# A fourth buffer of split weights in a two-layer decoder step, and attention's last copies moved ahead of the first output part

## The reference

```python
q = (xn @ wq).reshape(B, T, MEM_HEADS, MEM_HEAD_DIM)
s = jnp.einsum('bthd,bmhd->bhtm', q, k).astype(jnp.float32) * (MEM_HEAD_DIM ** -0.5)
p = jax.nn.softmax(s, axis=-1)
o = jnp.einsum('bhtm,bmhd->bthd', p, v).reshape(B, T, D_MODEL)
return o @ wo
...
for e in range(N_EXPERTS):
    out = out + combine[:, e:e + 1] * swiglu(xt, wg[e], wu[e], wd[e])
```

## Time and profile before

| | |
|---|---|
| the profiled execution | 1164.83 us, span 1163.0 us |
| three runs | 1159.54, 1162.23, 1162.55 us |
| TensorE (PE) busy | 1088.9 us, 94% |
| loading of stationary operands (PEld) busy | 1022.9 us, 88% |
| VectorE (DVE) busy | 794.7 us, 68% |
| ScalarE (ACT) busy | 646.4 us, 56% |
| read from memory | 265.83 MB, 234 GB/s over the span |
| mean granted clock of TensorE | 0.974 |

### The profile page before, as it was taken

How to read it: one execution, slowest core, us unless ns; L and a number is a source line. 1 busy time by engine, 2 the same in 40 slices (tenths; PEclk the granted TensorE clock), 3 DMA queues, 4 the chain that set the end, 5 groups by cost and what they waited for, 6 DMA issues and landing times.

```text
span 1163.0 us, 19968 instructions
## 1 busy us (share of the span) xinstructions
PE 1088.9 (94%) x7698; PEld 1022.9 (88%) x7698; DVE 794.7 (68%) x1121; ACT 646.4 (56%) x864; POOL 21.5 (2%) x40
## 2 busy tenths in 40 slices
PE   6999999899999998998997979999999999999995
PEld 5998987699999998998974979898989999999994
DVE  5598643566555656688623466887888788888883
ACT  5676543464434445675523336775766676676762
POOL 0001000000000000002100000000000000000000
PEclk8999999899999999999999869999999999999998
DMA  8444579746555554544498435996989698979961
GB/s 332 155 147 148 164 273 327 290 153 202 183 179 182 183 171 136 179 146 140 162 330 304 172 121 207 341 375 225 362 295 367 231 359 295 345 250 347 324 249 39
DMA packets 64276, 273.00 MB, mean 235 GB/s; under 512 B 7328, under 2 KB 7584, under 8 KB 63552
## 3 DMA queue, kind: packets, MB, share of 16 engines
q1 hardware_dynamic: 62352, 264.33, 64.2%
q0 software_dynamic: 1408, 7.12, 1.7%
q10 hardware_dynamic: 432, 0.38, 0.1%
HBM read 265.83 MB, written 5.98 MB: 234 GB/s over the span
## 4 chain that ended last, share of the span: by engine, by line
PE 71%; DVE 15%; ACT 7%; DMA 3%; issue 3%; SPq 0%; DVEq 0%; ACTq 0%
PE bank L598 10%; PE bank L595 10%; PE bank L600 10%; PE bank L599 10%; PE bank L596 10%; PE bank L597 10%; DVE wl L1402 4%; DMA ring<-dense 3%; ACT wh L1023 2%; PE bank L623 2%; DVE rstd L1397 2%; DVE wl L1663 2%; DVE sq L1413 1%; PE bank L754 1%; PE bank L878 1%
## 5 line engine op out<-in xcount | busy, mean ns | idle before, releaser
L1663 DVE TENSOR_TENSOR wl<-ring,wh 128x1408 fp32r<-128x1408 f32 x192 | 310.4, 1624 | 56.5 <-ACT wh L1269 56.3
L1402 DVE TENSOR_TENSOR wl<-ring,wh 128x1024 fp32r<-128x1024 f32 x170 | 207.1, 1224 | 198.4 <-ACT wh L1023 197.6
L1269 ACT ACTIVATE wh<-ring 128x1408 fp32r<-128x1408 f32 x189 | 261.0, 1381 | 82.2 <-PE bank L600 81.9
L595 PE MATMUL bank<-xh,wh 128*128 128x264 f32 x928 | 272.9, 294 | 21.3 <-DVE xl L1418 13.7
L1023 ACT ACTIVATE wh<-ring 128x1024 fp32r<-128x1024 f32 x170 | 178.9, 1056 | 172.1 <-PE bank L597 135.1
L596 PE MATMUL bank<-xl,wh 128*128 128x264 f32 x928 | 268.4, 289 | 0.0
L597 PE MATMUL bank<-xh,wl 128*128 128x264 f32 x928 | 267.6, 288 | 0.0
L599 PE MATMUL bank<-wh,xl 128*128 128x352 f32 (+4 forms) x736 | 243.1, 330 | 0.0
L595 PEld LDWEIGHTS bank<-xh,wh 128*128 128x128 f32 x928 | 179.6, 194 | 29.6 <-issue 25.1
L596 PEld LDWEIGHTS bank<-xl,wh 128*128 128x128 f32 x928 | 180.1, 194 | 0.0
L597 PEld LDWEIGHTS bank<-xh,wl 128*128 128x128 f32 x928 | 179.5, 193 | 0.0
(11 more groups left out here) (219 smaller groups left out, 1355.1 us busy)
## 6 DMA issues: line engine op xcount, KB each, us to landing
ring<-experts SPq DMA_DIRECT2D x192, 704.0 KB, 5.9
ring<-dense SPq DMA_DIRECT2D x234, 512.0 KB, 4.0
o_k<-kv POOLq DMA_DIRECT2D x2, 1024.0 KB, 4.5
o_v<-kv POOLq DMA_DIRECT2D x2, 1024.0 KB, 7.6
x<-xT SPq DMA_DIRECT2D x2, 528.0 KB, 4.9
o_y<-sq SPq DMA_DIRECT2D x4, 264.0 KB, 2.1
gatew<-gate_w POOLq DMA_DIRECT2D x2, 512.0 KB, 8.2
mem<-memT SPq DMA_DIRECT2D x1, 1024.0 KB, 13.3
```

The costliest lines, as they stand in the source:

```text
L595: mm(out, s_hi, m_hi, start=start, stop=False)
L1269: A(wh[:, jj % NBUF, :], eraw(jj % ESLOTS), ACT.Copy).then_inc(ehi_ready, 1)
L1402: V.tensor_tensor(wl[:, k % NBUF, 0:UNIT], raw(u), wh[:, k % NBUF, 0:UNIT].bitcast(F32), ALU.subtract)\
L1663: V.tensor_tensor(wl[:, jj % NBUF, :], eraw(jj % ESLOTS), wh[:, jj % NBUF, :].bitcast(F32), ALU.subtract)\
```

## The change

NBUF becomes 4. In the dense stages the memory of `wh` and `wl` stays as it was (three buffers of 1408 columns), now cut into four of 1024. In the expert stage the fourth buffer lies where `mem`, `poolw` and `gatew` were, which have done their service by then. Each `upto(k)` makes one part more than before; the one exception are calls whose bound is the first unit of `mo` (`first_mo`), which keep it. The call that made the first low part of `mo` ahead of `o8` is gone, so that part is made by the next call, behind L1624 to L1630.

```diff
-NBUF = 3
+NBUF = 4
...
-        wh = sb("wh", [P, NBUF, EUNIT], F32R)
-        wl = sb("wl", [P, NBUF, EUNIT], F32R)
+        wh = sb("wh", [P, 3 * EUNIT], F32R)
+        wl = sb("wl", [P, 3 * EUNIT], F32R)
+        assert NBUF * UNIT <= 3 * EUNIT
...
+        mixer_base = nc.sbuf_base
         mem = sb("mem", [P, KC, NM])
         poolw = sb("poolw", [P, RC, P])
         gatew = sb("gatew", [P, 2, RC, P])
+        assert nc.sbuf_base - mixer_base >= 8 * EUNIT
+        wh_last = nc.alloc_sbuf_tensor_at("expert_wh", [P, EUNIT], F32R, offset=mixer_base)
+        wl_last = nc.alloc_sbuf_tensor_at("expert_wl", [P, EUNIT], F32R, offset=mixer_base + 4 * EUNIT)
...
             def upto(self, k):
-                while self.at < min(k, NSPLIT):
+
+                while self.at < min(k if k in first_mo else k + 1, NSPLIT):
...
+        first_mo = [split[("mo", l, 0)] for l in range(DEPTH)]
...
-                        wait_used(act, max(k for k in range(NSPLIT) if k % NBUF == j))
+                        for b in range(j * EUNIT // UNIT, min(((j + 1) * EUNIT - 1) // UNIT + 1, NBUF)):
+                            wait_used(act, max(k for k in range(NSPLIT) if k % NBUF == b))
...
-                    while at[0] < min(k, EUNITS if last else EUNITS + NBUF):
+                    while at[0] < min(k + 1, EUNITS if last else EUNITS + NBUF):
...
                     read(V.tensor_tensor(xlo[:, m, 0:TP], bank(n)[:, 0:TP], xhi[:, m, 0:TP].bitcast(F32), ALU.subtract), n)
-                S.upto(start("mo", l) + 1)
                 n = tiles[("pvs", l)]
...
-                    while at[0] < min(k, EUNITS if last and side == 1 else EUNITS + NBUF):
+                    while at[0] < min(k + 1, EUNITS if last and side == 1 else EUNITS + NBUF):
```

More of the change, by code:

```diff
@@ L448, in eraw, with parts, eparts @@
             return ring[:, s * EUNIT:(s + 1) * EUNIT]
+        def parts(k):
+            b = k % NBUF
+            return [w[:, b * UNIT:(b + 1) * UNIT] for w in (wh, wl)]
+        def eparts(j):
+            b = j % NBUF
+            if b == NBUF - 1:
+                return wh_last[:, :], wl_last[:, :]
+            return [w[:, b * EUNIT:(b + 1) * EUNIT] for w in (wh, wl)]
         ends = {}
@@ L605, in unit @@
                 pe.wait_ge(slot_free[k % SLOTS], k // SLOTS + 1)
-                b = split[name] % NBUF
-                return [w[:, b, 0:UNIT].rearrange("p (k n) -> p k n", k=4) for w in (wh, wl)]
+                return [w.rearrange("p (k n) -> p k n", k=4) for w in parts(split[name])]
             def raw_unit(name):
@@ L914, in eunit @@
                     ewait(pe, eslot_free, j, v)
-                    return wh[:, j % NBUF, :], wl[:, j % NBUF, :]
+                    return eparts(j)
                 def group(g):
@@ L1022, in high_part @@
                     wait_used(act, k - NBUF)
-                A(wh[:, k % NBUF, 0:UNIT], raw(u), ACT.Copy).then_inc(hi_ready, 1)
+                A(parts(k)[0], raw(u), ACT.Copy).then_inc(hi_ready, 1)
             S = Splitter(high_part)
@@ L1245, in first_highs @@
                     if v0 == 0:
-                        wait_used(act, max(k for k in range(NSPLIT) if k % NBUF == j))
+                        for b in range(j * EUNIT // UNIT, min(((j + 1) * EUNIT - 1) // UNIT + 1, NBUF)):
+                            wait_used(act, max(k for k in range(NSPLIT) if k % NBUF == b))
                     else:
                         wait_full(act, *main.last("bD1"))
-                    A(wh[:, j, :], eraw(j), ACT.Copy).then_inc(ehi_ready, 1)
+                    A(eparts(j)[0], eraw(j), ACT.Copy).then_inc(ehi_ready, 1)
             first_highs(0)
@@ L1268, in ehigh @@
                 wait_eused(act, v, num, j - NBUF)
-                A(wh[:, jj % NBUF, :], eraw(jj % ESLOTS), ACT.Copy).then_inc(ehi_ready, 1)
+                A(eparts(jj)[0], eraw(jj % ESLOTS), ACT.Copy).then_inc(ehi_ready, 1)
             def gathered(num):
@@ L1401, in low_part @@
                 dve.wait_ge(hi_ready, k + 1)
-                V.tensor_tensor(wl[:, k % NBUF, 0:UNIT], raw(u), wh[:, k % NBUF, 0:UNIT].bitcast(F32), ALU.subtract)\
+                w_hi, w_lo = parts(k)
+                V.tensor_tensor(w_lo, raw(u), w_hi.bitcast(F32), ALU.subtract)\
                     .then_inc(slot_free[u % SLOTS], 1)
@@ L1662, in elow @@
                 dve.wait_ge(ehi_ready, EUNITS * vv + jj + 1)
-                V.tensor_tensor(wl[:, jj % NBUF, :], eraw(jj % ESLOTS), wh[:, jj % NBUF, :].bitcast(F32), ALU.subtract)\
+                w_hi, w_lo = eparts(jj)
+                V.tensor_tensor(w_lo, eraw(jj % ESLOTS), w_hi.bitcast(F32), ALU.subtract)\
                     .then_inc(eslot_free[jj % ESLOTS], 1)
```

## The result

| | before | after |
|---|---|---|
| median of 10 runs each | 1162.66 us | 1168.19 us |
| lowest and highest | 1158.95, 1167.58 | 1165.06, 1170.31 |
| span of the profiled execution | 1163.0 | 1166.8 |
| granted clock, mean | 0.974 | 0.971 |

The ratio is 1.0036, with a 95% interval from 1.002 to 1.0052 (the two medians alone would give 1.0048). The forecast was 1159.1 us, and the range ended at 1165.0, so both missed.

The account below looks back on a forecast made before the run. TensorE, busy 428 of 435 us over the expert stage, was taken as the bound; -1.6 - 3.7 + 1.6 + 3.4 - 2.8 = -3.1 us, on the median of 1162.23, gave 1159.1 us, range 1153.5 to 1165.

Parts of the forecast that it names:

- clock at the output projection: At attention's end, shorter TensorE idles were to cut the slow-clock loss: -2.8 us, bounds 0 and -4.5.
- waits for weight parts: TensorE's waits for low parts, dense 0.6 and experts 1.0 us, were to vanish: -1.6 us, between nothing and 2.1.
- query projection and half clock there: Next projection 0.8 us later in each attention (+1.6 in all), plus 1.7 us each for a slowed clock (+3.4).
- transfers behind it: Loads of the next keys, delayed by later scores freeing four ring slots: counted as nothing, at worst 1 us each.
- attention's last copies: After sample_values(3), copies no longer behind a low part: 1.99 us won, layer 1 1.73; -3.7 us, bounds -3.4 and -4.0.
- a ring slot comes free one step earlier: Query projection: parts made earlier move one 512 KB load from the full transfer stretch into the empty one, worth 1.3 us.
- T: Landing time of Q6's data in the query projection; taken to come 1.5 us earlier, bounds unchanged and 1.8 us earlier.
- Q6: The sixth query unit (index 6) in the query projection; its high part now stands before the second pair of query copies.
- The second, slower through the query projection: Rival, chance 0.17: Q6's landing does not move, each projection starts 2.3 us later; +4.7 us, 1166.9 us.
- The first rival: Blocked query-projection copies cost little: T 1.8 us earlier, clock falls at neither place; -8.8 us, 1153.4 us; chance 0.15.
- the third: Rival, chance 0.13: the idle at L803 becomes one at the first output product; within 1 us of today, 1162.
- The fourth: Rival, chance 0.05: the combine's repeating gaps in the expert stage were a lack of buffers; another -4.6, 1154.5 us.

## Why the prediction was wrong, by its own steps

Measured terms are steps between rows of the table, in the column after; they add up to the +3.75 at its end, which is the difference of the two profiled executions (the medians differ by 5.53). The forecast was -3.1, so 6.85 us were missed: 2.48 in the transfers, 1.39 at the start, 1.26 in the query projection with its clock, 1.26 in the clock at the output projection, and 0.46 in the rest.

| step of the prediction | forecast | measured |
|---|---|---|
| the start | not in the sum | +1.39 |
| waits for weight parts: 17.38 to 165.06, experts | -1.6 | -1.22 and -0.64 |
| query projection and half clock there | +1.6 and +3.4 | +2.79 and +3.47 |
| transfers behind it (174.44 to 211.07, 597.54 to 628.17) | 0, at worst 2 | +1.00 and +1.48 |
| attention's last copies | -3.7 | -1.53 and -1.74 |
| clock at the output projection | -2.8 | -0.36 and -1.18 |
| the rest (norms from 260 to 580, routing) | 0 | +0.66 and -0.37 |

*The step that failed first* is "a ring slot comes free one step earlier", from which I had T come 1.5 us earlier. It does not hold for Q6. The chain shows its load issued behind the scores of head 0, at 165.50 before and 165.67 after, both 3.07 us behind the start of those scores (162.43 and 162.60): the slot held cached keys, which TensorE frees itself, and no earlier weight part frees it sooner. The load took 5.70 us instead of 6.46, so T moved 0.8 us against the work around it, and in layer 1 0.1 (it lands at 591.91 + 5.76 = 597.67, and 595.08 + 2.73 = 597.81 would be unmoved). With T + 4.81 against T + 2.48 this gives 1.5 and 2.2 us, where I took 0.8 for each. The other half of the price was sized well: the scores took 3.49 and 3.54 us instead of 1.93, 3.2 us in all against the forecast 3.4. Together the two make 1.5 + 1.6 = 3.1 and 2.2 + 1.6 = 3.8, within 0.4 of the steps measured.

*The later transfers* I counted as nothing, on the ground that TensorE needs those loads only after a projection. The slots come free some 4.7 us later (SyncE goes on at 177.49 where the scores before ended at 172.74), in part since the half clock stretches the very scores that free them. In layer 0 the last head's keys were 1.47 us late, where nothing waited before, and the values 2.35, hardly more than the 2.27 before. In layer 1 the keys were 0.91 us late and the values 3.08, against 2.21 before. So the projection in between covered the loads only in part.

*The clock at the output projection.* I took the idle there for two pieces of 0.6 and 2.05 us. They are 0.71 and 2.65, in layer 1 0.72 and 3.27. The unit's load is issued while the last sample values still run, once a slot is free (213.46, 3.48 to landing). TensorE was done with them 2.19 us behind that issue, where it was 2.57 before (211.69 against 209.12), so a part of the longer wait comes from there. In layer 0 the half clock stayed: 0.50 from 220 to 224 and 0.88 in the next 4 us, where it was 0.50 and 0.89 before, each 4 us earlier. In layer 1 it was shorter: 0.57 from 648 to 652 alone, where the kernel before has 0.59 and 0.56 from 640 to 648. Layer 0 gave 0.36 us back, layer 1 1.18.

*The start* is a step that I left out. I looked at the extra part's buffer everywhere and at its data only in the query projection; the second place where the data are not there yet is the first microseconds.

*Weight waits and moved copies* came as forecast: -1.86 against -1.6, and -3.27 against -3.7, with L821 under 1 us in each layer. But 0.34 us of the first is the memory norm's wait for `hidden_lo` (1.42 us before, 1.08 after), which the sum did not count. "Nothing is added to either engine" was right and hid the point: the same wait at the same place is what the extra step keeps. In the old order the fourth buffer takes waits away, as at the memory norm.

*The rivals.* The second, slower through the query projection, is what happened; it gave +4.7 with T unmoved, 1 us of transfers and the slow clock staying, and its threshold of 2.65 us per attention was passed with 3.79 and 4.95 (the two steps together). That its total comes near the measured one is partly luck: it left out the start's 1.39 us and gave nothing for the clock at the output projection, where 1.54 were won. The reason it gave for T, the POOL queue's loads, is not what the rows show. I gave it 0.17 because I took T's move for likelier than its standing still, without looking at which instruction frees Q6's slot. The first rival fell with the 8.74 us behind Q6, the third with the 3.27 us that the moved copies won. The fourth fell: the combine's gaps are 2.5 and 2.1 us in all kernels with four buffers. The Trainium skill (Perfetto Trace Analysis, Optimization Strategy) says that repeating gaps can mean too few buffers, and also to find which instruction releases the gap; its second advice decided here.

## What to carry to other kernels

A buffer more and a step more ahead are two changes: the buffer lets the same copies wait for an earlier release, and the step spends that again. Before a copy is moved ahead in an engine's strict order, ask when its data land and which instruction frees the slot they land in, and then what stands behind it; an engine that looks idle for 9 us in front of a copy is harmless only while nothing urgent is queued behind it. Work that frees slots can cost twice when it is late: once itself, and once in the transfers that wait for it.

## What the runs showed of the hardware

In these rows the length of an idle of TensorE alone does not settle the clock behind it. In one execution a 3.63 us idle left the scores of head 1 at full clock (1.93 us), and a 3.81 us idle before the same instructions in the other layer halved it (3.64 us). In the kernels that moved Q6's parts, the other ten idles before these scores, of 3.49 to 4.58 us, were all paid too (scores of 2.80 to 3.64 us).

Shorter idles went either way. The two kernels with four buffers and the old order have the same code up to the sample values of layer 0. The one with the moved copies idled 2.15 us there and took 3.26 us, as shown above; the other idled 2.13 us and kept the full clock:

```profile
193.84 1.91 PE L782 MATMUL bank<-ring,work 128*8 128x256 f32 x32 [2.13 <-DMA ring<-dense]
```

So two profiles of the same code can differ by 1.35 us at one such place. The Trainium skill (TensorE: Matmul & The Clock Gate, Part 1) says that the number of slow matmuls at a kernel's start differs from run to run. No run here was read for that; these rows show the like in the middle of a kernel.
